# A chunked recurrence scan on one core: the order of its groups on every engine is rewritten

## The reference, cut to what matters

```python
def rwkv7_scan(f, d, s0, reverse):
    def step(state, inp):
        r_t, w_t, k_t, v_t, kk_t, a_t = inp
        sa = jnp.einsum('bhvk,bhk->bhv', state, -kk_t)
        state = (state * w_t[:, :, None, :] + sa[..., None] * (kk_t * a_t)[:, :, None, :]
                 + v_t[..., None] * k_t[:, :, None, :])
        return state, jnp.einsum('bhvk,bhk->bhv', state, r_t)
    ...
    s_last, ys = lax.scan(step, s0, xs, reverse=reverse)
    return s_last, jnp.moveaxis(ys, 0, 1)
```

## Time and profile before

| | us |
|---|---|
| median of three runs | 3581.45 |
| the profiled execution, its run | 3585.14 |
| its span from first to last instruction | 3583.3 |
| PE busy in the span | 3222.4 (90%) |
| DVE busy | 2218.8 (62%) |
| ACT busy | 1304.3 (36%) |
| POOL busy | 147.1 (4%) |

### The profile page before, as it was taken

One profiled execution on the slowest core, in us unless ns is written; L12 is line 12 of the kernel. 1 busy time (PEld: TensorE's weight loads), 2 busy tenths in 40 slices (PEclk: granted clock), 3 DMA queues, 4 the chain that ended last, 5 costly groups with the idle time before them and its releaser, 6 DMA issues. The chain is left out here.

```text
span 3583.3 us, 53773 instructions
## 1 busy us (share of the span) xinstructions
PE 3222.4 (90%) x21886; PEld 2576.1 (72%) x21886; DVE 2218.8 (62%) x3940; ACT 1304.3 (36%) x2245; POOL 147.1 (4%) x222
## 2 busy tenths in 40 slices
PE   6989999996999969986887889998999999889999
PEld 5767877654787758854665767887888777668787
DVE  7678866696688674676555646555666326653344
ACT  2243334324333332254434534222232435642243
POOL 0300000200000000000101200000000000000000
PEclk9989999998999989997997989999999999999999
DMA  7624453102333422110000022333233122022221
GB/s 299 170 95 176 188 176 112 61 35 65 115 136 140 141 76 95 68 68 29 3 32 10 3 73 95 118 118 110 102 145 126 53 87 68 1 70 92 81 103 66
DMA packets 64773, 340.78 MB, mean 95 GB/s; under 512 B 15120, under 2 KB 16656, under 8 KB 29072
## 3 DMA queue, kind: packets, MB, share of 16 engines
q1 hardware_dynamic: 61616, 325.51, 25.9%
q0 software_dynamic: 2048, 9.48, 0.8%
q10 hardware_dynamic: 864, 2.36, 0.2%
HBM read 326.53 MB, written 10.79 MB: 94 GB/s over the span
## 5 line engine op out<-in xcount | busy, mean ns | idle before, releaser
L265 DVE TENSOR_TENSOR weight_lo<-weight_ring,weight_hi 128x1024 fp32r<-128x1024 f32 x341 | 423.3, 1242 | 170.5 <-ACT weight_hi L250 165.6
L250 ACT CAST weight_hi<-weight_ring 128x1024 fp32r<-128x1024 f32 x341 | 355.9, 1044 | 158.3 <-PE banks L422 90.7
L420 PE MATMUL banks<-hT_hi.1,weight_hi 128*128 128x512 f32 x896 | 365.5, 408 | 25.7 <-PEq L383 23.5
L421 PE MATMUL banks<-hT_lo.1,weight_hi 128*128 128x512 f32 x896 | 358.3, 400 | 0.0
L422 PE MATMUL banks<-hT_hi.1,weight_lo 128*128 128x512 f32 x896 | 358.2, 400 | 0.0
L420 PEld LDWEIGHTS banks<-hT_hi.1,weight_hi 128*128 128x128 f32 x896 | 171.2, 191 | 68.7 <-issue 26.4
L421 PEld LDWEIGHTS banks<-hT_lo.1,weight_hi 128*128 128x128 f32 x896 | 171.2, 191 | 41.3 <-issue 1.9
L422 PEld LDWEIGHTS banks<-hT_hi.1,weight_lo 128*128 128x128 f32 x896 | 170.8, 191 | 41.7
L420 PE MATMUL banks<-hT_hi.3,weight_hi 128*128 128x512 f32 (+1 forms) x512 | 174.6, 341 | 0.0
L422 PE MATMUL banks<-hT_hi.3,weight_lo 128*128 128x512 f32 (+1 forms) x512 | 173.4, 339 | 0.0
L421 PE MATMUL banks<-hT_lo.3,weight_hi 128*128 128x512 f32 (+1 forms) x512 | 173.3, 339 | 0.0
(11 more groups left out here) (746 smaller groups left out, 7377.6 us busy)
## 6 DMA issues: line engine op xcount, KB each, us to landing
weight_ring<-ff SPq DMA_DIRECT2D x64, 1024.0 KB, 5.0
weight_ring<-ada SPq DMA_DIRECT2D x48, 1024.0 KB, 4.9
weight_ring<-up SPq DMA_DIRECT2D x44, 1024.0 KB, 6.9
weight_ring<-ada_ffn SPq DMA_DIRECT2D x24, 1024.0 KB, 4.9
weight_ring<-down SPq DMA_DIRECT2D x20, 1024.0 KB, 4.9
weight_ring<-ada_mix SPq DMA_DIRECT2D x16, 1024.0 KB, 4.9
first_blocks.1<-ada_mix SPq DMA_DIRECT2D x8, 1024.0 KB, 12.0
weight_ring<-cv_in SPq DMA_DIRECT2D x8, 1024.0 KB, 4.8
```

What stands on the lines that cost most here:

```text
L250: self.nc.scalar.copy(hi, raw).then_inc(self.hi_made, 1)
L265: self.nc.vector.tensor_tensor(lo, raw, hi.bitcast(F32), ALU.subtract).then_inc(self.lo_made, 1)
L420: nc.tensor.matmul(out, w_hi, x_hi, start=first, stop=False)
L421: nc.tensor.matmul(out, w_hi, x_lo, start=False, stop=False)
```

## The change

It changes the order of the calls in the four loops, and splits some of them so that they can stand apart. No instruction that computes is added or removed.

- PE: `x_t` is split into `x` (products) and `t` (transposes), still called together but for level order: `u(q)` and `y_from_state(q)` now come first, then levels 4 (now) and 1 (new) together, then `g_x(now, 4)`, and so on. `main_products(coming, 0)` moves in front of `g_x(new, 2)`; `main_products(., 1)`, which stood at the head of the next iteration, moves into the end of this one, before `g_x(new, 3)`; `z_from_chunk` and `z_from_state` no longer stand side by side.
- ACT: `copy_u` first; `start_inverse` and `factors(q + 4, 0)` move from behind `copy_v` to before `copy_xt(x, 5)`.
- DVE: `extend(x, 3)` (of level 3, now at the head of the next iteration) stands between the two halves of `start_extending`; `mask_ab` moves to the end of the iteration before; `new_state` moves behind `extend(new, 1)`.
- POOL: the gather of v moves behind the decay of b and k.

```diff
@@ gpsimd
                     for c in range(NCH):
-                        if c >= 1:
-                            pool.wait_ge(v_made, c)
-                        for d in range(2):
-                            nc.gpsimd.tensor_copy(v_now[:, d], v[:, :, tokens(d, c)]).then_inc(v_gathered, 1)
                         if c >= 2:
                             pool.wait_ge(bkt_made, c - 1)
...
                                 nc.gpsimd.tensor_tensor(to, src[:, js, tokens(d, c)], e[:, c % 2, 2, js, :], ALU.mult).then_inc(bk_decayed, 1)
+                        if c >= 1:
+                            pool.wait_ge(v_made, c)
+                        for d in range(2):
+                            nc.gpsimd.tensor_copy(v_now[:, d], v[:, :, tokens(d, c)]).then_inc(v_gathered, 1)
@@ scalar
+                        if q >= 0:
+                            copy_u(q)
                         if has_x:
                             copy_xt(x, 4)
-                        if q >= 0:
-                            copy_u(q)
                         if has_new:
                             copy_xt(new, 1)
+                        if q + 3 < NCH:
+                            start_inverse(q + 3)
+                        if q + 4 < NCH:
+                            factors(q + 4, 0)
                         if has_x:
                             copy_xt(x, 5)
                         if has_new:
                             copy_bk(new)
                             copy_v(new)
-                        if q + 3 < NCH:
-                            start_inverse(q + 3)
-                        if q + 4 < NCH:
-                            factors(q + 4, 0)
-                        if has_new:
                             copy_xt(new, 2)
@@ vector
                         if has_new:
-                            start_extending(new)
-                            mask_ab(new)
+                            start_extending(new, 0)
+                        if has_x:
+                            extend(x, 3)
+                        if has_new:
+                            start_extending(new, 1)
                             mask_ak(new)
+                            mask_r(new)
                         if has_x:
                             extend(x, 4)
+                        if coming < NCH:
+                            decayed_a(coming)
                         if has_new:
-                            mask_r(new)
+                            extend(new, 1)
                         if q >= 0:
                             new_state(q)
-                        if has_new:
-                            extend(new, 1)
                         if coming < NCH:
-                            decayed_a(coming)
+                            decayed_r(coming, 0)
+                            decayed_r(coming, 1)
                         if has_x:
                             extend(x, 5)
-                        if coming < NCH:
-                            decayed_r(coming)
                         if q >= 0:
                             add_y(q)
                         if has_new:
                             extend(new, 2)
+                        if coming < NCH:
+                            mask_ab(coming)
                         if has_x:
                             copy_z(x)
-                        if has_new:
-                            extend(new, 3)
@@ tensor, main_products
+                        pe.wait_ge(rc_made, 2 * c + d + 1)
                         if d == 0:
                             pe.wait_ge(a_made, 2 * c + 2)
-                            pe.wait_ge(rc_made, 2 * c + 2)
@@ tensor, the new loop (all lines replace those before; the guards are left out)
+                            u(q)
+                            y_from_state(q)
+                            x(now, 4)
+                            t(now, 4)
+                            x(new, 1)
+                            t(new, 1)
+                            g_x(now, 4)
...
                             s_products(q)
...
                             g_x(new, 1)
+                            x(now, 5)
+                            t(now, 5)
...
                             b_k_turned(new)
                             v_turned(new)
+                            x(new, 2)
+                            t(new, 2)
+                            g_x(now, 5)
...
                             y_from_chunk(q)
+                            main_products(coming, 0)
...
                             g_x(new, 2)
...
                             a(coming)
+                            z_from_chunk(now)
+                            x(new, 3)
+                            t(new, 3)
+                            z_from_state(now)
+                            main_products(coming, 1)
...
                             g_x(new, 3)
```

More of the change, by code:

```diff
@@ L2870, in decayed_a, with decayed_r, start_extending @@
                                                            in1=e[:, c % 2, 0, js, :], op0=ALU.mult, op1=ALU.mult).then_inc(a_made, 1)
-                    def decayed_r(c):
-                        if c >= 3:
+                    def decayed_r(c, d):
+                        if c >= 3 and d == 0:
                             dve.wait_ge(y1_made, c - 2)
[L2875 to L2886, removed]
+                        js = slice(2 * d, 2 * d + 2)
+                        dve.wait_ge(e_made, 6 * c + 3 * d + 2)
+                        nc.vector.tensor_tensor(AR_IN[c % 3][:, js, 1, :], r[:, :, tokens(d, c)], e[:, c % 2, 1, js, :], ALU.mult).then_inc(rc_made, 1)
+                    def start_extending(c, f):
+                        if f == 0:
+                            dve.wait_ge(g_init, c + 1)
+                            dve.wait_ge(main_made, c + 1)
+                        got = main_out[half[1 - f]].rearrange("p h (d f) m n -> p h d f m n", f=2)[:, :, :, f, 0, :]
+                        mask = level[half[1 - f], 0].unsqueeze(1).broadcast_to([HD, 2, 2, CH])
+                        nc.vector.copy_predicated(in_b_half(G[c % 3], f), mask, got).then_inc(extended[c % 2], 1)
                     def extend(c, l):
@@ L3017, in v_turned, with x @@
                         last.then_inc(v_made, 1)
-                    def x_t(c, l):
+                    def x(c, l):
                         if l == 1:
@@ L3028, in x_t, with t @@
                                                      start=True, stop=True)
+                    def t(c, l):
+                        pe.wait_ge(*extended_to(c, l))
                         for h in range(2):
@@ L3104, in _ @@
                     for q in range(-3, NCH):
[L3105 to L3110, removed]
+                        now, new, coming = q + 1, q + 2, q + 3
+                        has_now, has_new = 0 <= now < NCH, 0 <= new < NCH
                         if q >= 0:
@@ L3113, in _ @@
                             y_from_state(q)
-                        if has_x:
-                            g_x(x, 4)
+                        if has_now:
+                            x(now, 4)
+                            t(now, 4)
                         if has_new:
-                            x_t(new, 1)
+                            x(new, 1)
+                            t(new, 1)
+                        if has_now:
+                            g_x(now, 4)
                         if q >= 0:
                             s_products(q)
-                        if has_x:
-                            x_t(x, 5)
                         if has_new:
                             g_x(new, 1)
+                        if has_now:
+                            x(now, 5)
+                            t(now, 5)
+                        if has_new:
                             b_k_turned(new)
                             v_turned(new)
[L3126 to L3129, removed]
+                            x(new, 2)
+                            t(new, 2)
+                        if has_now:
+                            g_x(now, 5)
                         if q >= 0:
                             y_from_chunk(q)
+                        if coming < NCH:
+                            main_products(coming, 0)
                         if has_new:
@@ L3134, in _ @@
                         if coming < NCH:
-                            main_products(coming, 0)
                             a(coming)
+                        if has_now:
+                            z_from_chunk(now)
                         if has_new:
[L3138 to L3141, removed]
+                            x(new, 3)
+                            t(new, 3)
+                        if has_now:
+                            z_from_state(now)
+                        if coming < NCH:
+                            main_products(coming, 1)
                         if has_new:
```

## The result

The changed kernel takes 3546.86 us (median of four runs, 3543.68 to 3547.53), against 3581.93 for the kernel before (four runs of the same comparison). The ratio is 0.990, 95% interval 0.9883 to 0.9917: 35.1 us, or 1.0%, less. The prediction was 3547. The profiled execution has a span of 3541.9 us and a run of 3543.68; it is the fastest of the four.

What follows compares the result with a forecast made beforehand. TensorE bounds the scans, idling mainly 1.15 us an iteration for ScalarE's level 2 copy. Iterations go from 12.30 to 10.67 us; scans gain 18.2 and 16.4, together 34.6, taking the median from 3581.45 to 3546.8 us, range 3537 to 3563.

Steps and rivals of the forecast that it cites:

- (a): TensorE's wait at g_x(new, 2) for ScalarE's level 2 copy disappears, covered by main_products(coming, 0): 1.2 us gained an iteration.
- (b): On TensorE, x and t of level 3 now separate z_from_chunk and z_from_state: 0.16 us gained an iteration.
- (c): t(now, 5), b_k_turned and v_turned form one row of transposes, leaving five gaps of six: 0.17 us gained an iteration.
- (d): VectorE's extend of level 3 moves to the next iteration's head, before x of level 4: gain 0.1 us, margin 0.1.
- (e): State's round from z_from_state through copy_z to u stays hidden behind main products and g_x: cost zero, margin 0.35 us.
- (f): GpSimd's decays end more than 5 us early and its gather of v is early too: cost zero, a wait avoided.
- The sum: Steady iteration of the scan: 12.30 - 1.2 - 0.16 - 0.17 - 0.1 = 10.67 us.
- The beginning and the scans: First scan gains 18.2 us, 3.3 of it at its half-clock beginning; second gains 16.4, full clock again after 33 us.
- (A): Rival: TensorE's clock stays low longer in the scans; nine such iterations a scan give 3618 us; chance 0.05 for slower.
- (B): Rival: TensorE's margins of 0.04 to 0.35 us are used up; iteration 11.1 to 11.5, 3556 to 3563 us; chance 0.25.
- (C): Rival: the wait for ScalarE moves to g_x(now, 5) or main_products(coming, 0), 12.0 us an iteration, 3575 to 3581; chance 0.07.
- (D): Rival: TensorE's groups follow faster or clock rises early; iteration 10.4, 4 us from the clock, 3537; within forecast's 0.63.

Runs made afterwards that it cites:

- e2: Kernel before, with ScalarE's start_inverse and first factors moved before the copy of level 5: 3571.13 us, ratio 0.9961.
- e3: Kernel before, with both ScalarE's and GpSimd's new orders: 3563.98 us, ratio 0.9943.
- e4: Changed kernel, with ScalarE's start_inverse and first factors back behind the copy of v: 3551.94 us, ratio 0.9904.
- e6: Changed kernel, with main_products(coming, 0) back behind g_x(new, 2) on TensorE: 3550.43 us, ratio 0.99.
- e8: Changed kernel, with g_x(new, 1) put between the transposes of level 5 and those of b and k: 3551.92 us, ratio 0.99.
- e7: Changed kernel, with VectorE's extend of level 3 behind both halves of start_extending: 3551.32 us, ratio 0.9897.
- e1: Kernel before, with only GpSimd's gather of v moved behind its decay of b and k: 3583.15 us, ratio 0.9997.
- e5: Changed kernel, with GpSimd's gather of v back in front of its decays: 3570.51 us, ratio 0.995.
- e9: Changed kernel itself, run again beside the kernel before on another chip: 3542.5 us, ratio 0.9888.
- e11: Changed kernel reordered so both main_products(coming) stand side by side and product shapes change 15 times an iteration, not 17: 3540.19 us, ratio 0.9881.

## Why the prediction was right

Point by point, by its own steps:

- **The bound and its cause** (idle of TensorE in the scan, above all 1.15 us behind ScalarE's level 2 copy): shown by e2, where moving start_inverse and the first factors in ScalarE's queue shortens the iteration by 0.58, by e3, where GpSimd's part brings that to 1.05, and by the profile after, where TensorE has no idle left.
- **(a)** Gain 1.2, right, but its margin was mis-sized: 0.57, not 0.29. ScalarE's copies lie 0.48 us apart from start to start though each shows 0.59 (1763.20, 1763.68), which is 0.10 of the 0.15 by which that queue was earlier than in my walk, and TensorE reached the place 0.13 later. Hence e4 gave 0.45 for 0.75, and in e6 the cover of 0.65 us was hardly needed.
- **(b)** Right: no wait is left before z_from_state. By the distances it is a little more than 0.16: before, z_from_chunk took 0.84 us to the next start and z_from_state 0.25; after, z_from_chunk takes about 0.50 (0.84 together with x of level 3, which took 0.34 before) and z_from_state 0.39, 0.20 less in all. It was not tried alone.
- **(c)** The term was mis-sized, and the reading behind it too narrow. I saw the cost only as the 0.17 gap behind transposes and took the other changes at nothing. In the changed kernel a group of 16 small products takes 0.28 us to the next start in front of its own shape and 0.39 in front of another (1762.10, 1764.51), and two transposes take 0.27 or 0.37: some 0.1 us for any change of shape. Splitting the row of transposes again cost 0.33 in e8, where (c) has 0.17 for joining it; against that stands the one change between small shapes more that I left out of the sum. The rule of the Trainium skill ("TensorEngine Tiling (Array Packing)", Tiling Modes, Key Properties) that every change of mode drains TensorE agrees with these rows; they show the price, not the draining. My use of it was off: the changes into transposes also go from six to five, so with the costs equal 18 changes become 17, which gives 0.1, not nothing.
- **(d)** Right in place: no wait is left at x of level 4, and 0.3 us are lost in e7, where the two halves of start_extending stand together. The margin is 0.02, where I had 0.1. The gain of 0.1 was not tried alone, nor were the 0.9 us without u and y_from_state in between. VectorE waits 0.27 us for the main products before the first half of start_extending.
- **(e)** Right: copy_z ends at 1768.92, u starts at 1769.29.
- **(f)** Right, and the part that the profile of before shows least: e1 ratio 0.9997, e5 0.9 us an iteration.
- **The sum** of the iteration was 10.67; measured 10.59. Of the unseen neighbours, z_from_state in front of the main products costs 0.39 as one change of shape, and g_x in front of u only 0.29, since both have one shape.
- **The beginning and the scans**: first scan 19.0 us gained for 18.2. Second scan 23.9 for 16.4: I took the full clock at 33 us into it as before, and in this profile it came at about 13 (between 1912.88 and 1916.56, below). The profiled execution was forecast at 3550.5 and took 3543.68: it gained 41.5 us, the median 35.1. Of the other three executions only the mean granted clock is on record, 0.943 to 0.945 against 0.946 in the profiled one, and not when it rose. So the exact hit of the median is in part luck: the scans of the two profiles gained 42.9 us for the 34.6 forecast, and the late rise in the forecast stands in neither profile of the changed kernel. e9, with its ratio of 0.9888, would put the median at 3541.

The second scan's main products in the changed kernel, before and after the rise:

```profile
1912.88 1.23 PE L3000 MATMUL banks<-residual.1 64*128 64x128 f32 x8
...
1916.56 0.71 PE L3000 MATMUL banks<-residual.1 64*128 64x128 f32 x8
```

Of the rivals, (A) did not occur in any of the ten profiles with the new order of TensorE or a variant of it: the full clock came 24 us behind the first main product at the latest. (B) did not occur, the iteration being 10.59; what a margin that is used up costs is 0.3 us in e7. (C) is what e2 shows in small: the wait moves from ScalarE to GpSimd, and 0.40 of 1.15 us stays. Of (D), the clock's part came true in the profiled execution (7.5 us more than forecast in the second scan), the iteration of 10.4 did not.

## What to carry to other kernels

When one engine is the bound but still idles in a loop, write down start-to-start distances and hand-over latencies from one period, and walk all queues in the new order; that gave the iteration within 0.1 us, and its margins told which moves would hurt. An order that is worth nothing alone can be the next wait once the first is gone (GpSimd: 0 alone, 0.9 us an iteration at the end), so judge parts together, and expect waits on neighbouring groups to hide each other, not to add. Once no wait is left, group TensorE's work by shape: each change costs about 0.1 us here. And compare orders by their iterations too: e11 has the longer iteration and not the longer time, and in its profile the clock rose earlier.

## What the hardware showed that I had not expected

A change of the shape of products costs TensorE about 0.1 us also between small shapes (0.28 to 0.39 us for a group of 16), which is no row of idle time in the profile: it stands only in the distances. Consecutive copies on ScalarE start 0.48 us apart while each is shown 0.59 long. The clock of TensorE rose from 0.50 to 1.00 at very different distances from the first product of a scan: 33 us in the second scan before, 13 in the second scan after (in both profiles of that kernel), about 23 in the first scan of both kernels, and 10 in both scans of e4, e8 and e11. In e8 it fell once more for some 3 us, 0.63 in the window from 1709 to 1713 after 0.98 from 1703 to 1709. The one kernel with two profiles has the same distances in both, so the rise seems to go with the order of the groups and not with the execution, which two profiles don't prove. What decides it stays open.

GpSimd's order also touched VectorE. The decays of r (L2878), two inputs in SBUF, take 0.28 us each in e1, where GpSimd is idle beside them, and 0.35 and 0.55 in the kernel before, where GpSimd's decays of b and k, also with two inputs, run beside them. The first row is of the kernel before, the second of e1, which differs in GpSimd's order alone:

```profile
L2878 DVE TENSOR_TENSOR residual.1<-r.1,decay_factors.1 x16: 354/452/548, 1738.4 to 1825.0; 128x128 f32<-128x128 f32 x16
...
L2878 DVE TENSOR_TENSOR residual.1<-r.1,decay_factors.1 x16: 279/282/286, 1732.3 to 1818.7; 128x128 f32<-128x128 f32 x16
```

It changed nothing in the time of e1, since VectorE is not the bound there. In the changed kernel the decays of b and k fall beside extend and mask_ab of VectorE, as (f) says, and these take 0.45 and 0.41 us there, as long as without.
